# A Strassen decoder layer on eight cores: half of the second tile's gate-up operand sums and all sums of the down weights are made by GpSimd instead of VectorE, and stored by one transfer per group

## The reference

```python
proj = x @ w_in                                   # (B, S, 1536)
xp = proj[..., :512]
zg = gelu(proj[..., 512:])                        # u | v
pool_out = (pool(xp) @ pool_w) * pool_scale       # trailing means over 2/4/8/16, minus the token
sgu_out = u * (tril(W_s) @ LN(v) + b)             # chunks of 128 positions
h = LN(alpha * x + concat(pool_out, sgu_out) @ w_out)
gate, up = split(h @ w_gate_up)                   # D_FF = 2816
y = LN(alpha * h + (silu(gate) * up) @ w_down)
```

## Time and profile before

| | us |
|---|---|
| median of 3 runs (lowest, highest) | 2363.3 (2349.16, 2378.81) |
| the profiled execution's own time | 2356.65 |
| its span on the slowest core (core 6) | 2355.0 |
| spans of the eight cores | 2334.3 to 2355.0 |
| TensorE busy | 2233.0 (95%) |
| VectorE busy | 1504.5 (64%) |
| ScalarE busy | 966.3 (41%) |
| GpSimd busy | 213.7 (9%) |
| mean granted TensorE clock | 0.985 |

### The profile page before, as it was taken

One profiled execution on the slowest core, in us unless ns is written; L12 is line 12 of the kernel. 1 busy time (PEld: TensorE's weight loads), 2 busy tenths in 40 slices (PEclk: granted clock), 3 DMA queues, 4 the chain that ended last, 5 costly groups with the idle time before them and its releaser, 6 DMA issues.

```text
span 2355.0 us, 36012 instructions; the slowest of 8 cores (2334.3 to 2355.0 us)
## 1 busy us (share of the span) xinstructions
PE 2233.0 (95%) x10776; PEld 1024.0 (43%) x10776; DVE 1504.5 (64%) x2734; ACT 966.3 (41%) x1542; POOL 213.7 (9%) x306
## 2 busy tenths in 40 slices
PE   4989999889999999999999999999999999998997
PEld 1444344344444444444444444444444444444443
DVE  2578524897648746686457855588465864576465
ACT  2364410644316552174513744156431655136521
POOL 2021110300003000020001200020001200000001
PEclk9999999999999999999999999999999999998998
DMA  9958775898576455844568254763548545473543
GB/s 150 208 142 152 149 102 130 241 243 253 154 181 215 132 151 139 229 160 148 148 164 269 96 152 142 193 228 117 149 132 236 175 138 145 141 237 99 152 148 137
DMA packets 149596, 393.16 MB, mean 167 GB/s; under 512 B 15776, under 2 KB 44960, under 8 KB 149152
## 3 DMA queue, kind: packets, MB, share of 16 engines
q1 hardware_dynamic: 120240, 345.60, 46.1%
q0 software_dynamic: 29168, 45.26, 15.0%
HBM read 364.10 MB, written 71.96 MB: 185 GB/s over the span
## 4 chain that ended last, share of the span: by engine, by line
PE 81%; DMA 11%; issue 3%; DVE 2%; ACT 1%; POOL 1%; SPq 0%; DVEq 0%; ACTq 0%; POOLq 0%
PE ps L319 79%; DMA sb_xs<-xT 2%; DMA sb_hT<-sgu_bB 2%; DMA sb_h<-x 2%; DMA sb_ring<-scr_dn 1%; PE ps L657 1%; DMA out<-sb_h 1%; DMA sb_ring<-w_gate_up 1%; DMA sb_h<-w_down 1%; DMA scr_dn<-sb_h 1%; DMA scr_gu<-sb_ring 1%; DVE sb_h L330 1%; ACT sb_a L348 0%; ACT sb_junk L348 0%; SPq L80 0%
## 5 line engine op out<-in xcount | busy, mean ns | idle before, releaser
L319 PE MATMUL ps<-sb_hT,sb_ring 128*128 128x512 f16 x4928 | 1089.9, 381 | 33.4 <-DVE sb_a L324 12.9
L319 PEld LDWEIGHTS ps<-sb_hT,sb_ring 128*128 128x128 f16 x4928 | 478.2, 98 | 616.6 <-issue 62.2
L348 ACT ACTIVATE sb_xs<-ps 128x512 f32<-128x512 f32 x704 | 418.5, 597 | 398.8 <-PE ps L319 393.4
L319 PE MATMUL ps<-sb_ring,sb_a 128*128 128x512 f16 x2200 | 481.4, 379 | 1.0 <-DVE sb_h L331 1.0
L348 ACT ACTIVATE sb_junk<-sb_h,sb_st 128x1024 f16<-128x1024 f32 x128 | 146.8, 1147 | 654.1 <-DVE sb_st L336 648.2
L319 PEld LDWEIGHTS ps<-sb_ring,sb_a 128*128 128x128 f16 x2200 | 215.1, 98 | 260.9 <-issue 1.8
L331 DVE SCALAR_TENSOR_TENSOR sb_h<-sb_h,ps 128x512 f32<-128x512 f32 x256 | 172.5, 686 | 231.9 <-PE ps L319 221.1
L324 DVE TENSOR_TENSOR sb_a<-ps,sb_xs 128x512 f16<-128x512 f32 x352 | 241.9, 687 | 37.8 <-PE ps L319 37.1
L324 DVE TENSOR_TENSOR sb_a<-sb_a,sb_xs 128x512 f16<-128x512 f16 x352 | 146.3, 422 | 187.2 <-ACT sb_xs L348 176.8
L319 PE MATMUL ps<-sb_xs,sb_ring 128*128 128x512 f16 x1024 | 224.6, 379 | 0.3 <-ACT sb_hT L348 0.3
L324 DVE TENSOR_TENSOR sb_xs<-ps,sb_xs 128x512 f32<-128x512 f32 x176 | 121.4, 690 | 148.9 <-PE ps L319 147.7
(11 more groups left out here) (66 smaller groups left out, 1451.3 us busy)
## 6 DMA issues: line engine op xcount, KB each, us to landing
sb_ring<-scr_gu SPq DMA_DIRECT2D x132, 512.0 KB, 4.3
sb_ring<-scr_gu SPq DMA_DIRECT2D x132, 384.0 KB, 3.3
sb_ring<-scr_dn SPq DMA_DIRECT2D x98, 512.0 KB, 4.5
sb_h<-x SPq DMA_DIRECT2D x64, 512.0 KB, 7.9
out<-sb_h SPq DMA_DIRECT2D x64, 512.0 KB, 8.6
sb_ring<-scr_dn SPq DMA_DIRECT2D x49, 384.0 KB, 4.4
sb_ring<-scr_in SPq DMA_DIRECT2D x36, 512.0 KB, 7.4
sb_xs<-xT POOLq DMA_DIRECT2D x16, 1024.0 KB, 15.9
```

Of the source, the lines that this page charges most:

```text
L319: ins = t.matmul(o, lhsT=l, rhs=r, start=s0, stop=s1, skip_group_check=True)
L348: return a.activation(out=out, in_=in_, func=func, **kw)
```

## The change

Three edits. In the second tile (`mt == 1`) blocks 4 and 6 of each gate-up group are summed by GpSimd, with a planned duration of 1.1 us instead of 0.42. In `dn_prep` all four sums of each group are GpSimd's, planned at 1.1 us instead of 0.34. And the seven stores of a `dn_prep` group become one transfer of 896 KB; the blocks keep the buffer's order in `scr_dn`, so `DN_SUM` maps a product to its block, and a product's load now depends on whole groups. The number of sums does not change.

```diff
@@ start (gate-up)
+                    e = "dve" if mt == 0 else "pool"
-                    tt(bl(4), bl(0), bl(6), ALU.subtract, bkk(0) + bkk(6), bkk(4), d)
+                    tt(bl(4), bl(0), bl(6), ALU.subtract, bkk(0) + bkk(6), bkk(4), d if mt == 0 else 1.1, eng=e)
                     tt(bl(2), bl(3), bl(0), ALU.subtract, bkk(3) + bkk(0), bkk(2), d)
-                    tt(bl(6), bl(1), bl(2), ALU.subtract, bkk(1, 2), bkk(6), d)
+                    tt(bl(6), bl(1), bl(2), ALU.subtract, bkk(1, 2), bkk(6), d if mt == 0 else 1.1, eng=e)
@@ dn_strassen
+        DN_SUM = (0, 1, 2, 4, 5, 3, 6)
-                ss = [chunk_load(scr_dn[prod, :, k0 * 512:k1 * 512], (k1 - k0) * 512,
-                                 [("scr_dnp", prod, k) for k in range(k0, k1)]) for k0, k1 in ((0, 4), (4, 8), (8, 11))]
+                ss = [chunk_load(scr_dn[DN_SUM[prod], :, k0 * 512:k1 * 512], (k1 - k0) * 512,
+                                 [("scr_dnp", k) for k in range(k0, k1)]) for k0, k1 in ((0, 4), (4, 8), (8, 11))]
@@ dn_prep
-                d = D2(512)
-                tt(v(4), v(3), v(0), ALU.subtract, kk(3) + kk(0), kk(4), d)
...
-                for p_, i in ((0, 0), (1, 1), (2, 2), (5, 3), (3, 4), (4, 5), (6, 6)):
-                    S.dma("sp", scr_dn[p_, :, k * 512:(k + 1) * 512], v(i), reads=kk(i),
-                          writes=[("scr_dnp", p_, k)], nbytes=131072)
+                d = 1.1
+                tt(v(4), v(3), v(0), ALU.subtract, kk(3) + kk(0), kk(4), d, eng="pool")
...
+                S.dma("sp", scr_dn[:, :, k * 512:(k + 1) * 512].rearrange("q p c -> p q c"),
+                      v(0, 7).rearrange("p (q c) -> p q c", q=7), reads=kk(0, 7), writes=[("scr_dnp", k)], nbytes=917504)
```

More of the change, by code:

```diff
@@ L960, in dn_prep @@
                       writes=kk(0, 4), nbytes=1 << 20)
-                d = D2(512)
-                tt(v(4), v(3), v(0), ALU.subtract, kk(3) + kk(0), kk(4), d)
-                tt(v(5), v(2), v(4), ALU.subtract, kk(2) + kk(4), kk(5), d)
-                tt(v(3), v(2), v(3), ALU.subtract, kk(2) + kk(3), kk(3), d)
-                tt(v(6), v(1), v(5), ALU.subtract, kk(1) + kk(5), kk(6), d)
-                for p_, i in ((0, 0), (1, 1), (2, 2), (5, 3), (3, 4), (4, 5), (6, 6)):
-                    S.dma("sp", scr_dn[p_, :, k * 512:(k + 1) * 512], v(i), reads=kk(i),
-                          writes=[("scr_dnp", p_, k)], nbytes=131072)
+                d = 1.1
+                tt(v(4), v(3), v(0), ALU.subtract, kk(3) + kk(0), kk(4), d, eng="pool")
+                tt(v(5), v(2), v(4), ALU.subtract, kk(2) + kk(4), kk(5), d, eng="pool")
+                tt(v(3), v(2), v(3), ALU.subtract, kk(2) + kk(3), kk(3), d, eng="pool")
+                tt(v(6), v(1), v(5), ALU.subtract, kk(1) + kk(5), kk(6), d, eng="pool")
+                S.dma("sp", scr_dn[:, :, k * 512:(k + 1) * 512].rearrange("q p c -> p q c"),
+                      v(0, 7).rearrange("p (q c) -> p q c", q=7), reads=kk(0, 7), writes=[("scr_dnp", k)], nbytes=917504)
         def drain(g):
```

## The result

The changed kernel takes 2383.14 us (median of 19 runs), the kernel before 2361.21 beside it. Their ratio is 1.0094, with a 95% interval from 1.0070 to 1.0118: a loss of 16.5 to 27.9 us. That is less than the 2% taken here as the least that counts, but the interval leaves out 1, so the sign is clear. The profiled execution took 2374.88 us, its span on core 6 was 2373.0.

A forecast was written before the change was run, and what follows sets the result against it. TensorE, busy for 95% of the span, was taken as the bound, so only its stalls or lower clock due to VectorE could be won. Terms +5 - 1.5 = +3.5 us on a median of 2363.3 gave 2367 us, range 2343 to 2396.

The forecast's parts named there:

- five signs: Second tile's gate-up 145 to 157 us, gaps ended by GpSimd, late transposes, sum near 1.25 us, `dn_prep` some 15 us later.
- Start of gate-up, +5: Second tile: z-row factor queues behind GpSimd's load and sums, so the in stage's transposes end about 5 us later.
- Gate-up, -1.5: Second tile's gate-up: VectorE's gaps go, GpSimd's blocks come late by 7.2 us; 150.8 us in all, -1.5 us.
- The sum's price, 1.25 us: One 128x512 sum on GpSimd takes 1.25 us, from its commonest two-input instruction; 88 make 110 us.
- The single store, 0: `dn_prep`: one transfer in place of seven stores moves the same bytes and changes the time by 0.
- the first: Rival: GpSimd keeps up, z rows and gate-up blocks in time, gate-up about 141 us; -15 us, 2348; chance 0.20.
- The second: Rival: GpSimd and VectorE block each other, GpSimd's sums take 1.7 us; +12 more, 2379; chance 0.17.
- against that end: Objection to the blocking rival's slow end near 2411: only VectorE's norm steps and scans take over 0.7 us.
- What VectorE was to save: 88 sums at 0.34 us, 30 us, leave VectorE's queue, and with them its waits for `w_down`.

The follow-up runs named there:

- e4: Changed kernel, each of the 88 GpSimd sums replaced by eight zero fills that read nothing from SBUF: second tile's gate-up 141.1 us, ratio to before 0.9882.
- e3: Kernel before with only the single 896 KB store per down group, all sums on VectorE: second tile's gate-up 154.3 us, ratio to before 0.9963.
- e7: Changed kernel, each GpSimd sum replaced by a copy of its first operand, one SBUF input: second tile's gate-up 153.1 us, 8.4 idle; no ratio.
- e1: Changed kernel with gate-up blocks 4 and 6 summed by VectorE again, down sums on GpSimd: second tile's gate-up 166.2 us, ratio to before 1.0089.
- e2: Kernel before with only gate-up blocks 4 and 6 on GpSimd in the second tile: its gate-up 153.8 us, ratio to before 0.9935.
- e5: Changed kernel with the second tile's first-norm steps held back into gate-up: that stage 171.2 us, 25.9 idle; no ratio.

## Why the prediction was right or wrong

The forecast was +3.5 us, the loss was some 22 (ratio 1.0094 of 2361.21). The range held it and "within 2%" was right, but by luck: the terms of the sum didn't come out, and the part of the range that held the loss had been put there for longer sums on GpSimd's queue. Of the five signs that were to show it right one came, the price of a sum; gate-up wasn't between 145 and 157 us, none of its gaps was ended by GpSimd, the transposes weren't late, and `dn_prep`'s last store went out at 582.1, 42 us later and not 15.

*Start of gate-up, +5:* it didn't come. The step that failed here is "the load waits for the first tile's output rows to leave `sb_h`, which nothing here hastens": the load of group 1 went out at 432.85 instead of 438.65, the sums still ran alone at 1.14, and the product that releases the z rows ended at 451.1, not 455.2. The transposes had no gap; out and in gained 2 us.

*Gate-up, -1.5:* it was +24.1 (medians of the cores), and this is where the forecast broke. The step that failed is "I take VectorE's gaps in gate-up as gone, apart from 1.5 us at its start, where the operand sums of `sb_hT` are made by VectorE as before". They were not made as before. That start alone has a gap of 20.10 us. The operand sums began 11.7 us after the stage, before 1.3 ahead of it: 13.0 late. From 457 to 492 us thirteen two-input instructions and a pair of scalings on VectorE were longer than undisturbed, by 13.3 us in all; then five operand sums and a ring sum by 0.95 each, 5.7: together 19.0, what the gap there grew by (20.1 against 1.1 before). In e4, with the same order and no waits, the gap is 1.30. The blocks on which I had spent the term, late at groups 6, 7 and 9 for want of `w_down`, were never waited for.

*The sum's price, 1.25 us:* 1.14 alone, 1.36 and 1.45 as means, near enough. It was the wrong engine's price. *The single store, 0:* some 3 to 4 us in e3. Its landing was as before; that the changed order is the reason is likely but wasn't tested.

*The rivals:* GpSimd kept up, as the first said, and nothing was gained by it. The second had the mechanism and, at 2379, nearly the time, but by another road: it charged GpSimd's sums with 0.45 us each along GpSimd's queue, and its test (VectorE's sums longer) was the one that came true. GpSimd's sums were far from 2 us on average, but not where the gap arose: there four in a row took 8.01 [485.25 in GpSimd's timeline]. Its point "against that end" was that few VectorE instructions take over 0.7 us. That weighs what GpSimd waits for and not what VectorE does: beside a sum of 1.16 us even a 0.16-us instruction takes 1.12. The prediction said of the mutual exclusion that it "also holds the other way about, which no row of this trace shows", and set no price on it. It is the Trainium skill, "SBUF — State Buffer", section "Who interferes with whom", that says so; e4 and e7 agree, writes alone leaving VectorE's two-input instructions at 0.42 and 0.675 us and a single read lengthening them. A bound from above was to be had from rows: 88 x 1.25 = 110 us on VectorE's queue, if each sum meets a two-input instruction.

*What VectorE was to save:* 30 us left its queue, and it was busy for 16 us more in all, so some 46 came back as waits inside its instructions. In the stage it was busy for 144.68 us instead of 124.17, with 59 instructions fewer.

What stays open: the change's 22.6 us of added idle time are 7.7 more than e1's and e2's together. How much of that is more meetings of the two engines and how much order wasn't told apart; e5 gives about 5 us to order.

## What to carry to other kernels

Handing work from VectorE to GpSimd isn't free where both read SBUF and VectorE has two inputs there: charge each GpSimd instruction's length to VectorE's queue as well, unless VectorE then reads PSUM or stands idle; here 0.34 us saved cost up to 0.95. Before moving work off a crowded engine, look for work on it that is early: holding back sixteen norm steps by a dependence gave what the offload was after (the stage fell by 7 us). Cutting the other engine's instructions shortened each wait here but multiplied their number, and the price then fell on that engine's queue.

## What the runs showed of the hardware that was not expected

A full wait of VectorE is GpSimd's instruction less about 0.2 us (0.95 for 1.16, 0.41 for 0.61, 0.23 for 0.39) and doesn't depend on VectorE's own length: 128x16 and 128x1024 paid the same. With work queued on both sides the two engines often take turns, as 1.57 us for each of four on either side shows. That is no rule, though: in e2 (core 7) one norm step lasted until two of GpSimd's sums were over, 2.19 us longer than its 1.27. VectorE's and GpSimd's timelines:

```profile
458.94 3.46 DVE L330 SCALAR_TENSOR_TENSOR sb_h<-sb_h,sb_st,sb_g1B 128x1024 f32<-128x1024 f32 x1
...
459.04 2.26 POOL L324 TENSOR_TENSOR sb_ring<-sb_ring 128x512 f16<-128x512 f16 x2
```

And a scaling with one tensor input, `sb_a<-sb_hT,sb_stv`, grew as well (0.54 before, 0.92 in the change), and in e4, where GpSimd filled instead of summing, too (0.75); why isn't shown. The sums that read PSUM never did: their means are 0.68 to 0.69 us in every run.
